# A two-layer encoder trunk in compensated float32: straight layers, gate slots of five k tiles, ScalarE's last result, and the weights' low part in two instructions

## The reference

```
x <- LN1(alpha*x + 0.5*SwiGLU_1(x))
x <- LN2(alpha*x + W_out[concat(PoolMix(u), RWKV7(z))]),   [u | z] = x W_in
h  = alpha*x + 0.5*SwiGLU_2(x)
x <- LN3(h + sigmoid(h W_g + b_g) * (p[i] W_ple))
```

## Time and profile before

| | us |
|---|---|
| median of three runs | 2998.16 (2995.62 to 3004.26) |
| the profiled execution's own time | 3005.33 |
| its span, first to last instruction | 3003.5 |
| PE busy | 2725.9 (91%) |
| POOL busy | 1447.4 (48%) |
| DVE busy | 1091.3 (36%) |
| ACT busy | 696.7 (23%) |

### The profile page before, as it was taken

The page is one execution under the profiler, slowest core; times in us unless marked ns, Lnnn a source line. Parts: engine busy times, 40 slices in busy tenths (PEclk is TensorE's granted clock), DMA queues, the critical chain, the costliest instruction groups (busy, mean ns, idle before and its releaser), DMA issues.

```text
span 3003.5 us, 68153 instructions
## 1 busy us (share of the span) xinstructions
PE 2725.9 (91%) x27640; PEld 2615.4 (87%) x27640; DVE 1091.3 (36%) x1448; ACT 696.7 (23%) x1193; POOL 1447.4 (48%) x932
## 2 busy tenths in 40 slices
PE   8999989888887899999799999798888878999995
PEld 8999979877777799999699999797777778999994
DVE  3222037645553422212432210575555434222125
ACT  3221021234421322200232210212343213221013
POOL 5555546523314455555555556455223145555553
PEclk9999999889997999999899999997999989999998
DMA  4222312100001122322222223220000012222321
GB/s 146 91 84 88 90 56 89 37 3 4 4 17 51 56 88 87 95 86 75 85 71 90 85 87 90 60 85 24 3 4 4 17 57 70 84 91 89 90 74 58
DMA packets 64117, 192.63 MB, mean 64 GB/s; under 512 B 11712, under 2 KB 14016, under 8 KB 63936
## 3 DMA queue, kind: packets, MB, share of 16 engines
q1 hardware_dynamic: 59904, 185.95, 20.0%
q10 hardware_dynamic: 4032, 4.08, 0.4%
HBM read 186.88 MB, written 3.12 MB: 63 GB/s over the span
## 4 chain that ended last, share of the span: by engine, by line
PE 81%; issue 7%; DVE 5%; POOL 3%; ACT 3%; DVEq 0%; DMA 0%; ACTq 0%; POOLq 0%; SPq 0%
PE ps L519 64%; PE ps L575 8%; PE ps L534 3%; PE ps L679 1%; POOL w_lo L464 1%; DVE xl L1192 1%; PE ps L603 1%; PE ps L694 1%; PE ps L663 1%; POOL w_hi L462 1%; PE ps L622 1%; DVE y L1188 1%; PE ps L746 1%; DVE rs L1177 0%; ACT xh L887 0%
## 5 line engine op out<-in xcount | busy, mean ns | idle before, releaser
L519 PE MATMUL ps<-xh,w_hi 128*128 128x272 f32 x4032 | 849.5, 292 | 105.9 <-POOL w_lo L464 49.1
L464 POOL TENSOR_TENSOR w_lo<-w_raw,w_hi 128x1024 fp32r<-128x1024 f32 (+3 forms) x380 | 855.2, 2251 | 31.7
L519 PE MATMUL ps<-xl,w_hi 128*128 128x272 f32 x4032 | 839.0, 290 | 0.0
L519 PE MATMUL ps<-xh,w_lo 128*128 128x272 f32 x4032 | 836.9, 289 | 0.0
L462 POOL TENSOR_SCALAR w_hi<-w_raw 128x1024 fp32r<-128x1024 f32 (+3 forms) x380 | 375.5, 988 | 864.8 <-PE ps L519 853.5
L519 PEld LDWEIGHTS ps<-xh,w_hi 128*128 128x128 f32 x4032 | 638.4, 190 | 119.7 <-DVE xl L1192 55.8
L519 PEld LDWEIGHTS ps<-xl,w_hi 128*128 128x128 f32 x4032 | 641.0, 191 | 0.0
L519 PEld LDWEIGHTS ps<-xh,w_lo 128*128 128x128 f32 x4032 | 637.2, 190 | 0.0
L1144 DVE TENSOR_TENSOR hf<-sg,ps 128x544 f32<-128x544 f32 x88 | 63.5, 722 | 707.7 <-PE ps L519 707.7
L519 PE MATMUL ps<-hh,w_hi 128*128 128x272 f32 x1472 | 305.4, 289 | 0.0
L519 PE MATMUL ps<-hl,w_hi 128*128 128x272 f32 x1472 | 303.7, 287 | 0.0
(11 more groups left out here) (242 smaller groups left out, 3186.9 us busy)
## 6 DMA issues: line engine op xcount, KB each, us to landing
w_raw<-in_w1i SPq DMA_DIRECT2D x88, 512.0 KB, 3.5
w_raw<-in_w2i SPq DMA_DIRECT2D x88, 512.0 KB, 3.5
w_raw<-in_wz SPq DMA_DIRECT2D x44, 512.0 KB, 3.5
w_raw<-in_w1o SPq DMA_DIRECT2D x32, 448.0 KB, 3.3
w_raw<-in_w2o SPq DMA_DIRECT2D x32, 448.0 KB, 3.3
w_raw<-in_w1o SPq DMA_DIRECT2D x16, 512.0 KB, 3.5
w_raw<-in_wo SPq DMA_DIRECT2D x16, 512.0 KB, 3.5
w_raw<-in_w2o SPq DMA_DIRECT2D x16, 512.0 KB, 3.5
```

The lines of the kernel that those rows point to most:

```text
L464: pool.tensor_tensor(w_lo[k][:, 0:nk, :], w_raw[k][:, 0:nk, :], w_hi[k][:, 0:nk, :].bitcast(F32), ALU.subtract).then_inc(w_split, 1)
L519: mm = pe.matmul(ps[:, 2 * pair + h, 0:HT], w[:, j, :], x[:, k0 + j, h * HT:(h + 1) * HT], start=(part == 0 and j == 0 and q == 0), stop=( ...
```

## The change

- The layer loop is written out on all engines (`for l in range(DEPTH)`), and in the heads and elsewhere the counts are constants; `to_reg` and `constants_there` in front of them go, as do a few waits of POOL and VectorE that stood between a register and its use. ScalarE's loop over the gate tiles is also written out.
- The low part is made in two instructions, the first WF = 3 k tiles (w_first) and the rest (w_split). PE starts a slot at w_first and waits for w_split before the fourth k tile. The refill of w_raw still waits for w_split.
- The gate stage gets slots of five k tiles from a concatenated array: gate tiles 0 to 4, then gate tiles 5 to 7 with embedding tiles 0 and 1. A new function `gates` replaces the special cases in `dense`. A new semaphore gate_mm rises after the gate's last matmul, and the sigmoid waits for that.
- In the last norm ScalarE writes the result (y plus bias) into sqs, which is stored from there. xh, xl, alpha*x and VectorE's sum are left out for this norm.
- In `half_a`, ScalarE does a one-column sigmoid (`early`) at place 0; VectorE's piece 5 is moved ahead of `step` at place 4. In `half_b`, PE's waits of place 5 are moved behind `chunk_in` and `step`.

```diff
-          ("f2i", FT, [8, 8]), ("f2o", 4, [8, 7, 7, 8, 7, 7]), ("gp", 4, [4, 4, 2, 4, 4, 2])]
+          ("f2i", FT, [8, 8]), ("f2o", 4, [8, 7, 7, 8, 7, 7]), ("gp", 4, [5, 5, 5, 5])]
...
-            with pool.Fori(0, DEPTH) as l:
+            for l in range(DEPTH):
...
-                            pool.tensor_tensor(w_lo[k][:, 0:nk, :], w_raw[k][:, 0:nk, :], w_hi[k][:, 0:nk, :].bitcast(F32),
+                            pool.tensor_tensor(w_lo[k][:, 0:WF, :], w_raw[k][:, 0:WF, :], w_hi[k][:, 0:WF, :].bitcast(F32),
+                                               ALU.subtract).then_inc(w_first, 1)
+                            pool.tensor_tensor(w_lo[k][:, WF:nk, :], w_raw[k][:, WF:nk, :], w_hi[k][:, WF:nk, :].bitcast(F32),
                                                ALU.subtract).then_inc(w_split, 1)
...
+            def three(pair, k, j, x_hi, x_lo, kx, start, stop):
+                for q, (w, x) in enumerate(((w_hi[k], x_hi), (w_hi[k], x_lo), (w_lo[k], x_hi))):
+                    for h in range(2):
+                        mm = pe.matmul(ps[:, 2 * pair + h, 0:HT], w[:, j, :], x[:, kx, h * HT:(h + 1) * HT],
+                                       start=(start and q == 0), stop=(stop and q == 2))
+                return mm
+
+            def gates(l, hi, lo, ready, base):
+                def body(m, first):
+                    for i in range(4):
+                        k, part = i % 2, i % 2
+                        n = l * SLOTS + SLOT0["gp"] + m * 4 + i
+                        if part == 0:
+                            pe.wait_ge(tile_out[0], out_count(l, "gp", m * 2 + i // 2) - 1)
+                        pe.wait_ge(w_first, n + 1)
+                        for j in range(5):
+                            if j == WF:
+                                pe.wait_ge(w_split, n + 3)
+                            c = 5 * part + j
+                            pair, x_hi, x_lo, kx = (0, hi, lo, c) if c < 8 else (1, hh, hl, c - 8)
+                            if c == 8:
+                                pe.wait_ge(tile_out[1], out_count(l, "gp", m * 2 + i // 2) - 1)
+                                if first and i == 1:
+                                    pe.wait_ge(pl_ready, l * 2 + 2)
+                            if first and i < 2 and c < 8:
+                                pe.wait_ge(ready, base + c + 1)
+                            mm = three(pair, k, j, x_hi, x_lo, kx, c in (0, 8), c in (7, 9))
+                            if c == 7:
+                                mm.then_inc(gate_mm, 1)
+                        mm.then_inc(slot_used, 1)
...
-                        pe.wait_ge(w_split, n + 3)
+                        pe.wait_ge(w_first, n + 1)
                         for j in range(nk):
+                            if j == WF:
+                                pe.wait_ge(w_split, n + 3)
...
-                due, blocks = pe.to_reg(n * NSTEP + s), pe.to_reg(n * 5 + (2, 5)[g])
-                constants_there()
+                due, blocks = n * NSTEP + s, n * 5 + (2, 5)[g]
...
-                            due, due_bonus = pe.to_reg((n - 1) * 3 + 1 if norm_before else n + 2), pe.to_reg(n + 2)
-                            constants_there()
-                            if norm_before:
-                                pe.wait_ge(hn_newton, due)
...
                         step(k - 3, 1, n)
                     if 5 <= k < 9:
+                        if k == 5:
+                            due, due_bonus = (n - 1) * 3 + 1, n + 2
+                            if norm_before:
+                                pe.wait_ge(hn_newton, due)
+                            if nxt:
+                                pe.wait_ge(bonus_ready, due_bonus)
...
+                    if last:
+                        act.activation(sqs[:, m, :], y[:, m, :], ACT.Identity, bias=col(l, b + m)).then_inc(fin_ready, 1)
+                        continue
...
+                    if nxt and k == 0:
+                        act.activation(early[:, :], eps[:, 0:1], ACT.Sigmoid)
...
-                with act.Fori(0, 4) as m:
+                for m in range(4):
                     for k in range(2):
-                        act.wait_ge(slot_used, used_count(l, "gp", 6 * m + (3 * k + 1)))
+                        act.wait_ge(gate_mm, l * 8 + 2 * m + (k + 1))
...
+                    if nxt and k == 4:
+                        prepare_1(l, p + 1, 5, not right)
                     if left and k >= 3:
                         step(k - 3, 0, n)
...
-            for m in range(KT):
-
-                dve.tensor_tensor(y[:, m, :], xh[:, m, :].bitcast(F32), xl[:, m, :].bitcast(F32), ALU.add).then_inc(fin_ready, 1)
```

More of the change, by code:

```diff
@@ L30 @@
 NU = 9
+WF = 3
 ALPHA = (2.0 * DEPTH) ** 0.25
@@ L106, in build @@
         eps = sb("eps", [P, 2])
+        early = sb("early", [P, 1])
         lora_all = sb("lora_all", [P, DR])
@@ L503, in body @@
                             pe.wait_ge(tile_out[pair], out_count(l, name, tile) - 1)
-                        if name == "gp" and i == 2 and first:
-                            pe.wait_ge(pl_ready, l * 2 + 2)
-                        pe.wait_ge(w_split, n + 3)
[L509 to L512, removed]
+                        pe.wait_ge(w_first, n + 1)
+                        k0 = (0, 8, 15)[part]
                         for j in range(nk):
+                            if j == WF:
+                                pe.wait_ge(w_split, n + 3)
                             if first and pair == 0 and i < per:
                                 pe.wait_ge(ready, base + k0 + j + 1)
[L517 to L521, removed]
+                            mm = three(pair, k, j, hi, lo, k0 + j, part == 0 and j == 0, part == per - 1 and j == nk - 1)
                         mm.then_inc(slot_used, 1)
@@ L819, in half_b @@
                         normalise(l, p - 1, k, nxt, True)
-            with pe.Fori(0, DEPTH) as l:
+            for l in range(DEPTH):
                 dense(l, "f1i", xh, xl, xl_ready, l * 40)
@@ L877, in norm @@
                 inst = l * 3 + which
+                last = inst == 3 * DEPTH - 1
                 for m in range(KT):
@@ L1049, in half_b @@
                         normalise(l, p - 1, k, nxt)
-            with act.Fori(0, DEPTH) as l:
+            for l in range(DEPTH):
                 ffn(l, 0, "f1i")
@@ L1151, in residual @@
                     dve.memset(ysum[:, :], 0.0).then_inc(sum_ready, 1)
-                due = dve.to_reg(inst * 8 + 8)
-                dve.wait_ge(loaded, 16 * NLOAD)
-                dve.wait_ge(ax_ready, due)
+                dve.wait_ge(ax_ready, inst * 8 + 8)
                 per = 3 if name in ("f1o", "f2o") else 1
@@ L1363, in half_a @@
                         chunk_out(k - 1, l, p - 1)
-                    for q in IN_A.get(k, ()) if nxt else ():
+                    for q in IN_A.get(k, ()) if nxt and k != 4 else ():
                         prepare_1(l, p + 1, q, not right)
@@ L1383, in half_b @@
                         normalise(l, p - 1, k, nxt)
-            with dve.Fori(0, DEPTH) as l:
+            for l in range(DEPTH):
                 ffn(l, 0, "f1i")
@@ L1438, in _ @@
                 norm(l, l * 3 + 1, l * 40 + 24, COL["ln2_g"], COL["ln2_b"])
-                due = dve.to_reg((l + 1) * (NPAIR * 32))
-                dve.wait_ge(loaded, 16 * NLOAD)
-                dve.wait_ge(wkv_stored, due)
+                dve.wait_ge(wkv_stored, (l + 1) * (NPAIR * 32))
                 ffn(l, 1, "f2i")
```

50 lines of the change are left out of this document (18 added, 32 removed).

## The result

The changed kernel takes **2928.16 us** (median of 4 runs, 2918.27 to 2930.84) against 2998.83 us before (4 runs, 2995.62 to 3004.26) on the same chip: ratio 0.976, 95% interval 0.9734 to 0.9787. That is 70.7 us where 38 were forecast, outside the range. The profiled executions lie further apart, 3005.33 and 2918.27 us (spans 3003.5 and 2916.5), because the one of after was the fastest of its runs; what makes such runs differ turned out to be a part of the answer.

What follows compares the result with a forecast made beforehand. PE held 81% of the chain of waits, issue 7%; the terms summed to -38.2 us, taking the profiled 3005.3 to 2967.1 and the median to 2960, with an 8-in-10 range of 2943 to 2979.

Steps and rivals of the forecast that it cites:

- The heads of layer 0 have 42 pieces of 0.14 on the chain: Heads: constant counts shorten hand-overs to PE from 0.14 to 0.04 us; -6 us, bounds 0 and -14.
- the heads pay in full: Rival, 0.18: all 0.14 pieces and sequencer pieces in the heads go, -14 for -6; 2950 us.
- The moved places: Heads: early sigmoid takes a table load out of the way, -3.0 us; VectorE's piece 5 and PE's moved waits, 0 each.
- PE isn't in it: Heads: the chain at PE's moved Newton-step wait runs through VectorE, POOL and ScalarE; 0 us, bounds 0 and -6.
- What the second instruction costs: Norms and starts of wo: splitting POOL's low part delays VectorE; +3.2 and +1.8, together +5.0 us.
- The exclusion by which I reckoned: Rule behind the +5.0: VectorE instructions with two SBUF inputs and GpSimd instructions reading SBUF exclude each other for whole instructions.
- The tail of z: End of z: PE goes on after the first low piece; -1.3 us a layer, -2.6 in all (0 to -7).
- The start: Program start: with three k tiles first, PE begins at 12.0 instead of 13.74; -1.7 us, bounds 0 and -1.8.
- The gate stage: Gate tiles: five-k-tile slots remove gaps of 1.08 us a tile; 6.7 us a layer, -13.4, bounds 0 and -15.2.
- The end: Last norm: without xl, alpha*x and sums, eight y follow at 0.70 us each; -15.0 us, within 1 either way.
- Straight layers at the boundary: Layer boundary: written-out layers remove POOL's unexplained pause of 1.77 us before w_hi; -1.5 us.
- the slower rival: Rival, 0.04: the mid-slot wait drains PE, 0.167 us in each of 364 slots; +60 us, 3020 us.

Runs made afterwards that it cites:

- Straight layers alone: Kernel before with only the layer loops written out and counts made constants on all five engines: 2970.32 us, ratio 0.9903.
- after's second profile: Profile from measuring the changed kernel once more, unchanged, in a later group: 2923.77 us, ratio 0.9739.
- one piece: Changed kernel with each low part of the weights made in one instruction again: 2933.99 us, ratio 0.9779.

## Why the prediction was wrong

**The direction was right, and most parts did what the prediction said of them; the sum failed mainly in the heads**, by one term that I didn't have and two that I sized too small. Straight layers alone brought 26 us in the medians, where the prediction had 7.5 for them (6 in the heads, 1.5 at the boundary).

- *"The heads of layer 0 have 42 pieces of 0.14 on the chain ... I take -6, a bit under the middle."* This step failed. Straight layers alone shortened the heads by 27.3 us, and by 13.4 with the clock taken out at 0.37 (16 at 0.30), the far end of my bounds (0 and -14) or past it. The doubt whether 0.10 was the weight load and not the register is answered: the hand-overs behind constants are 0.04. The rival "the heads pay in full" had this right and still stopped at 2950.
- *The clock in the heads* was in no term. Before, PE's half clock at the heads' start lasted some 30 us; I read the clock only at the program's start and in the tail of z. With constant waits it was back after some 12 us in both layers of the profile; with the tail of layer 0's heads that is 44.4 us less of half clock, an estimated 13 to 16 us of time. That part is not sure in every execution: in layer 1 of after's second profile the half clock lasted 29 us again. I had seen as a list of costs that add up, where a change in the waits can also change the speed of what lies between them.
- *The moved places*: -3.0 was forecast, 7.8 measured. One by one: early sigmoid 4.4 for 3.0, PE's waits 3.2 where I had 0 with a bound of -6, piece 5 1.6 for 0. A layer's part of each (2.2, 1.6, 0.8) is hardly more than the 1.9 by which the two layers of one kernel differ, or less, so only the sum is safe. "PE isn't in it" was probably wrong for the moved waits.
- *"What the second instruction costs: +5.0."* Measured about 0 or less (the later norms and the starts of wo differ by -0.3 to +0.65 us between one piece and two, and by both signs; up to the first z two pieces are 2.7 us shorter). In the first norm the Newton step did spread over two short blocks, as forecast: 1.50 and 1.40 us instead of 2.75 and a short one. But the stages with the norms aren't longer for it. The exclusion by which I reckoned isn't contradicted: VectorE's operations still take 1.3 to 1.5 us each beside POOL's, and 0.73 alone. What failed is my addition of the delays; which of them is hidden, and behind what, no run shows.
- *The tail of z*: -1.3 a layer forecast, -2.7 and -4.2 measured against the same kernel with one piece. PE's pause is 2.4 us and not 4.1, and in layer 1 the clock stayed at 1.00 through it, where it fell in layer 0. I had named that as the bound (-7) and not taken it. The z stage took 143.5 us with that fall and 142.0 without it, the same step of 1.5 us as a dip in the heads.
- *The start*: first matmul at 11.83 us for 12.0 forecast, partly by luck. Straight layers alone moved it from 13.74 to 13.00, which no term had, and the first piece then gave 1.04 (12.87 with one piece) where 1.7 was forecast. *The gate stage*: tiles 7.51 us apart and one table load, as forecast; f2 and gate together gave -10.3 in layer 0, of which straight layers alone gave 2.2, so the gate stage is 8.1 for 6.7. *The end*: gate and end together -23.5 for -21.7, and 9.2 us from the first y to the end of the span for 9 to 10. *Straight layers at the boundary*: POOL's pause of 1.77 us is gone (w_hi starts at 1451.72, as the sum of squares ends) and the stage lost 2.2 us against 1.5.
- *The steady stretches* kept their pace (392.37 us for 3132 matmuls, 0.1253 each, in the first feed-forward stretch of after's second profile, with the second wait in each slot), so the slower rival is dead.
- *From profile to median*: the profiled 87 us are 71 in the medians. After's profiled execution was 10 us under its own median; the second profile of the same kernel shows 8 us of such a difference in layer 1's heads, by a longer half clock at their start and three dips.

Left open: why the half clock mostly ends sooner behind constant waits, and what part of that and of the 13.4 us comes from constant waits on PE and what from those on VectorE, ScalarE and POOL. Register waits on PE alone were not tried. Of the 13.4 us, 84 hand-overs at 0.10 make 8.4; that the rest is the other engines' sequencers is argued, not shown. Outside the heads, straight layers alone gave about 5.5 us (2.5 of it up to the first z), which I can't place instruction by instruction.

## What to carry to other kernels

Look at the granted clock stretch by stretch before summing up waits: where PE runs at half clock for 30 us behind a pause, each us of it was worth 0.30 to 0.37 us here, and an edit that shortens waits there can change the clock as well. Replace counts in registers by constants where the chain is made of many short hand-overs, even at the cost of a longer program. And run-to-run differences of 5 to 10 us can come from the clock alone, so judge an edit of a few us by stages cut at the same instructions, with the clock taken out, in more than one profile of each kernel.

## What the hardware showed that I had not expected

- A hand-over to PE behind a constant wait takes 0.04 us, behind a wait on a register's value with its constant wait in front 0.14. Replacing all of them, on every engine, shortened the heads by an estimated 13.4 us with the clock taken out.
- A single dip of the clock inside a pair of heads costs 1.5 us and falls in some pairs and not in others of the same program: 49.3 and 50.8 us. The half clock at the heads' start, too, lasts 12 or 29 us in one and the same program.
- Busy matmuls in the pause put the half clock off, but don't always prevent it: on the kernel before they cut it from 30 to 10 us, on the one after they only moved it.
- VectorE's hl operation in the feed-forward parts fell from 2250 to 1024 ns in the mean with POOL's low part cut in two (2392 in the kernel after with one piece), and PE's list of waits doesn't name it:

```profile
L1176 DVE TENSOR_TENSOR hl<-hf,hh 128x544 f32 x88 | 90.1, 1024 | 82.5 <-ACT hh L898 82.5
```
